# Moving the memory side of two cross-attentions into the block before them, its second layer's share into the recurrence's chunk loop

## The chip, the cores and the metric

The kernel runs on one core of a Trainium2 chip. The metric is the device time of one execution in microseconds (us); lower is better. Engines are named as in the profile: PE (TensorE), PEld (its weight loads), DVE (VectorE), ACT (ScalarE), POOL (GpSimd, which issues most of the small DMAs here) and SP (SyncE, which issues the stream of weights).

## The reference, cut to what matters

Two networks run one after the other on 256 tokens of width 2048. The second has two layers; each has a mixer, a cross-attention to a fixed memory of 256 rows, and a feed-forward part.

```
for layer in range(2):
    xn = rms_norm_2(x, norm_mix[layer])
    mix = even block (sparse attention + rwkv7) @ even_w_out   if layer == 0
          s5 block @ odd_w_out                                 if layer == 1
    x = x + mix
    x = x + memory_cross_attention(rms_norm_2(x, norm_xattn[layer]),
                                   rms_norm_2(mem, norm_mem[layer]), wq, wkv, wo)
    x = x + squared_relu_mlp(rms_norm_2(x, norm_ffn[layer]), w_up, w_down)

def memory_cross_attention(xn, memn, wq, wkv, wo):
    q  = (xn @ wq)        # 256 x 512
    kv = (memn @ wkv)     # 256 x 1024: keys and values, 4 heads of 128 each
    ...softmax attention of q over kv...
    return o @ wo
```

`memn @ wkv` depends on the inputs alone: not on x, nor on anything computed earlier.

## The kernel before, in words

**Weights.** Each large product is a `Gemm`: chunks of 512 output columns (`c`), two tiles of 128 tokens (`t`), and slots (`s`) of 256 rows of weights. SP streams the slots of all Gemms in the order of the list `gemms` (`ORDER`) into a ring of 8 (`ring`, 512 KB each, L524), eight ahead of their use. A slot has two halves: SP writes the raw weights into half 1. For a Gemm with `split=True`, ACT (`round_hi`, L1409) writes a rounded copy into half 0 and DVE (`take_lo`, L2017) the rest into half 1, and PE makes three products of each block: high by high, high by low and low by high (L841). With `split=False` PE makes one float32 product from the raw half, and half 0 of the slot isn't used.

**Streams.** ACT and DVE walk through a Gemm with `stream`: at each slot `s` of chunk `c` they round or split the slot that lies 8 ahead; at the last slot, `s == g.slots - 1`, they first call a hook that empties the accumulation banks of chunk `c` (`empty` on ACT, `hook` on DVE, as in `residual`, L2150).

**The even block.** After its input product come three small float32 Gemms (`uq`, `qidx`, `uv`), the sparse attention (`dsa_units`; the index scores are at L1112, and DVE then picks the top 64 by eight rounds of MAX8), and the recurrence `rwkv`. DVE first mixes each token with the one before (`w_sh`, shifted copies that POOL loads by DMA, L2742 to L2748), then come two passes over 128 tokens (low-rank products L1135, running sums L1140, exponentials, transposes L896), the gate (L1158, L1159), and the 32x32 matrices of all 8 chunks of 32 tokens, which DVE inverts (the solve, L2836 to L2844). Last is the loop over the 8 chunks (`heads`, L1171): PE and DVE hand each other z, u and the state, and PE's products all have 32 or 64 rows and columns. Then comes `even_out`, a split Gemm.

**The cross-attention `xat(l)`.** PE runs `xq` (one chunk, 8 slots, split); POOL has loaded the memory (`memb`), ACT sums its squares, DVE scales a diagonal by the inverse root (`norm_diag`), and PE turns the memory with it (`turn_normed`, L898, 64 products of 128x128), DVE and ACT splitting the result into `feat`. Then PE runs `xkv` (two chunks, 16 slots, split: 192 products of 128x512), turns q and k (L896), and attends. `xo` brings the result back to x. The attention waits for the semaphore `xqk_ready`, which ACT raises behind its whole stream (L1834).

Of the kernel before, what the change touches and what calls it, by code (L numbers as in the profile page):

```python
# [30 lines left out]
ACT = mybir.ActivationFunctionType  # L31
# [5 lines left out]
P = 128  # L37
# [6 lines left out]
KS = 2  # L44
# [132 lines left out]
def two_blocks(nc, I, out):  # L177
    ctx = ExitStack()
    with ctx:
# [74 lines left out]
        q_d = dram("q_d", (2 * SEQ, B1_HALF))  # L254
        s_bd = dram("s_bd", (4, P, 2048))
# [43 lines left out]
        memb = view(20480, TT, D)  # L299
        diag = view(30464, TT, P)  # L300
# [54 lines left out]
        g.append(Gemm("uv", flat(W("dsa_w_uv_2", 0)), 256, chunks(0, 1024), 2, "act_free", split=False))  # L355
        g.append(Gemm("even_out", W("even_w_out_2", 0), D, chunks(0, D), 2, "dve_free", unroll=True))
# [61 lines left out]
        d_ckt = view(29984, 2, SEQ)  # L418
        d_kid = view(0, TT, P)
# [156 lines left out]
        def _(pool):  # L576
# [51 lines left out]
            for l in range(2):  # L628
# [24 lines left out]
                dma(gates[l][0:8, 0], g_d[l].rearrange("j c d -> (j c) d"), "g8_in")  # L653
# [6 lines left out]
            pool.wait_ge(sem("x_norm_even"), L.due("x_norm_even"))  # L660
# [8 lines left out]
            pool.wait_ge(sem("even_h"), L.due("even_h"))  # L669
            pool.wait_ge(sem("dsa_part"), L.due("dsa_part", 5))  # L670
# [20 lines left out]
            dma(w_g2a[:, 0], I["rwkv_g2_2"][0, 0:P], "g2_in")  # L691
            dma(w_g2a[0:32, 1], I["rwkv_g2_2"][0, P:160], "g2_in")
# [22 lines left out]
            for o in range(2):  # L715
                dma(w_tt[64 * o:64 * o + RC], by_unit[o], "t_in")
# [16 lines left out]
            for l in range(2):  # L733
                if l == 1:
# [4 lines left out]
                    pool.wait_ge(sem("x_norm_odd"), L.due("x_norm_odd"))  # L739
# [15 lines left out]
                pool.wait_ge(sem("mem_free"), L.due("mem_free"))  # L755
                dma(memb, I["mem_2"][0].rearrange("(t p) d -> p t d", p=P), "mem_in")
# [5 lines left out]
        def _(pe):  # L762
# [161 lines left out]
            def turn_normed(src, tiles=TT, on=diag):  # L924
# [111 lines left out]

            def block1(l):
# [6 lines left out]
                pe.wait_ge(sem("sgu_in"), 16 * (l + 1))  # L1044
# [20 lines left out]
                pe.wait_ge(sem("g8_in"), 16 * (l + 1))  # L1065
# [15 lines left out]
            def even():  # L1081
                g_in, g_uq, g_qi, g_uv, g_out = gemms["even"]
# [19 lines left out]
                for t in range(TT):  # L1102
# [3 lines left out]
                    for h in (0, 4):  # L1106
                        turn([d_qi[:, t, (h + j) * P:(h + j + 1) * P] for j in range(4)])
                pe.wait_ge(sem("dsa_part"), E.due("dsa_part"))
                for t in range(TT):
                    for hp in range(8):  # L1110
                        bank = begin("act_free")
                        pe.matmul(bank[:, :], d_qit[:, hp, t * P:(t + 1) * P], d_kit, start=True, stop=True) \  # L1112
                            .then_inc(sem("unit_full"), E.up("unit_full"))
                pe.wait_ge(sem("bias_ready"), E.due("bias_ready"))
# [11 lines left out]
            def rwkv():  # L1126
                pe.wait_ge(sem("rwkv_in"), 16 * 7)
                for t in range(TT):
# [17 lines left out]
                    mm.then_inc(sem("unit_full"), E.up("unit_full"))  # L1146
                    pe.wait_ge(sem("arbk_ready"), E.due("arbk_ready"))
# [3 lines left out]
                pe.wait_ge(sem("g2_in"), 32)  # L1151
# [35 lines left out]
                within(0)  # L1187
                for c in range(NRC):
# [11 lines left out]
                    if c == 0:  # L1200
                        pe.wait_ge(sem("t_in"), 32)
# [5 lines left out]
                    heads("act_free", lambda hp, o: state(hp, o, 1) + [(w_G[c % 2][two[o], hp, 1, :], kbv[two[o], 1, hp, :])])  # L1207

            def xat(l):
                g_q, g_kv, g_o = gemms[f"xat{l}"]  # L1210
                g_prev = gemms["odd" if l else "even"][-1]
                gemm(g_q, feat_lhs(feat), parts=True, between=(3, lambda: turn_x(g_prev, x4, 3)))
                turn_normed(memb)
                gemm(g_kv, feat_lhs(feat), parts=True)
                pe.wait_ge(sem("xqk_ready"), E.due("xqk_ready"))
                for t in range(TT):
                    turn([xa_q[:, t, j * P:(j + 1) * P] for j in range(4)])
                    turn([xa_kv[:, t, j * P:(j + 1) * P] for j in range(4)])
# [45 lines left out]
            def odd():  # L1264
# [3 lines left out]
                def turn_end():  # L1268
                    turn_x(g_prev, x4, 3)
                    E.seen["rstd_ready"] = 3  # L1270
# [112 lines left out]
        def _(act):  # L1383
# [28 lines left out]
            def stream(g, empty=None, counts=(), unroll=False, each=None):  # L1412
# [4 lines left out]
                def chunk(c, i):  # L1417
                    for s in range(g.slots):
                        if s == g.slots - 1 and empty:
                            empty(c, i)  # L1420
# [211 lines left out]

            def s5_natural():
# [101 lines left out]
            def even():  # L1735
                g_in, g_uq, g_qi, g_uv, g_out = gemms["even"]

                def to_hb(c, cs, t, bank):
# [12 lines left out]
                    .then_inc(sem("act_free"), E.up("act_free")))  # L1751
                evac(g_qi, lambda c, cs, t, bank: f(d_qi[:, t, c * CH:(c + 1) * CH], bank, ACT.Copy) \
# [11 lines left out]
                act.nop().then_inc(sem("kt_ready"), E.count("kt_ready"))  # L1764
                slots = [stage[:, 0], stage[:, 1], prob[:, 0], prob[:, 1]]
# [7 lines left out]
                act.wait_ge(sem("rl_used"), E.due("rl_used", 4))  # L1773
                attend(dsa_units())

                for t in range(TT):
                    if t == 0:
# [5 lines left out]
                        .then_inc(sem("lora_ready"), E.up("lora_ready"))  # L1783
                    skip("unit_full", 4)
# [15 lines left out]
                    f(w_t[:, 0], w_t[:, 0], ACT.Exp, scale=-DECAY).then_inc(sem("eexc_ready"), E.up("eexc_ready"))  # L1800
                act.wait_ge(sem("kbv_out"), E.due("kbv_out", 16 * 6 * TT))
# [8 lines left out]
                for c in range(NRC):  # L1810
# [1333 lines left out]
```

## Time and profile before

| | |
|---|---|
| median of 3 runs | 4608.1 us (4605.08 to 4614.41) |
| the profiled execution's own time | 4608.53 us, span 4606.7 us, 1.8 us around it |
| PE busy | 4047.0 us, 88% of the span |
| DVE / ACT / POOL busy | 2283.0 / 1666.4 / 134.4 us |
| mean granted TensorE clock | 0.922 |
| DMA | 717.12 MB, mean 156 GB/s |

The page gives busy time by engine and, in 40 slices of 115 us, shares and the granted clock. A timeline gives instructions in order; its bracket is the idle time of that engine ahead of them and what ended it. One float32 product of 512 columns shows as two records. Times inside the span count from its start.

### The profile page before, as it was taken

Reading aid. Unit: us, or ns where it says so; the run is one execution under the profiler, and the core shown is the slowest. Engines: PE = TensorE matmul, PEld = TensorE weight load, DVE = VectorE, ACT = ScalarE, POOL = GpSimd, SP = SyncE. Lnnn points to the kernel's source line nnn. Section 1 sums busy time; section 2 is a strip of 40 time slices with the busy share of each in tenths; the row PEclk is TensorE's granted clock in tenths of the full one; section 3 lists DMA queues with packets and bytes.
Section 4 is the critical chain, followed back from the end, with each engine's and each line's share of the span. In section 5 each row is a group of like instructions: output and inputs, shape, how many; then the busy total and the mean of one; then the engine's idle time right before and its main releaser. Section 6 shows DMA issues by size and latency. Waiting matters only on the chain. (4 is left out here: it accounts for less than half of the span.)

```text
span 4606.7 us, 52925 instructions
## 1 busy us (share of the span) xinstructions
PE 4047.0 (88%) x21471; PEld 3175.4 (69%) x21471; DVE 2283.0 (50%) x3339; ACT 1666.4 (36%) x2235; POOL 134.4 (3%) x241
## 2 busy tenths in 40 slices
PE   6699999699798999633878999999986898999999
PEld 3466657568687787322657788788875777887887
DVE  6611223553555654665365555455546455554554
ACT  4121212331343443310024454354442454543543
POOL 1000000000000000012100000000000000000000
PEclk8899999899999999855689999999988999999999
DMA  9465554213364375221145466665651554666665
GB/s 355 182 209 196 201 179 136 69 69 95 101 202 126 102 215 176 72 72 40 30 129 169 132 185 190 183 186 188 225 175 52 174 178 129 186 188 183 187 197 163
DMA packets 350199, 717.12 MB, mean 156 GB/s; under 512 B 24270, under 2 KB 26666, under 8 KB 344602
## 3 DMA queue, kind: packets, MB, share of 16 engines
q1 hardware_dynamic: 331872, 637.74, 44.9%
q0 software_dynamic: 17600, 76.35, 5.0%
q8 instruction: 145, 2.38, 0.2%
q14 instruction: 62, 0.51, 0.0%
q10 hardware_dynamic: 520, 0.14, 0.0%
HBM read 686.33 MB, written 24.38 MB: 154 GB/s over the span
## 5 line engine op out<-in xcount | busy, mean ns | idle before, releaser
L2017 DVE TENSOR_TENSOR ring_r<-ring,ring_r 128x1024 fp32r<-128x1024 f32 (+1 forms) x1016 | 1231.7, 1219 | 1835.7 <-ACT ring_r L1409 1816.4
L1409 ACT ACTIVATE ring_r<-ring 128x1024 fp32r<-128x1024 f32 (+1 forms) x1016 | 1065.8, 1054 | 1987.8 <-DMA ring<-in_w_in 656.0
L841 PE MATMUL acc<-ring_r,feat_hi 128*128 128x512 f32 x5376 | 1689.6, 396 | 53.4 <-DVE big L2150 17.0
L841 PEld LDWEIGHTS acc<-ring_r,feat_hi 128*128 128x128 f32 x5376 | 1011.4, 190 | 318.6 <-DVE ring_r L2017 42.0
L841 PE MATMUL acc<-ring_r,feat_lo 128*128 128x512 f32 x2688 | 1055.6, 393 | 0.0
L841 PE MATMUL acc<-ring_r,hid_t_hi 128*128 128x512 f32 x2048 | 631.5, 389 | 0.0
L841 PEld LDWEIGHTS acc<-ring_r,feat_lo 128*128 128x128 f32 x2688 | 510.0, 190 | 109.1
L841 PEld LDWEIGHTS acc<-ring_r,hid_t_hi 128*128 128x128 f32 x2048 | 383.7, 188 | 79.3
L841 PE MATMUL acc<-ring_r,hid_t_lo 128*128 128x512 f32 x1024 | 398.5, 389 | 0.0
L841 PE MATMUL acc<-ring_r,feat_e_hi 128*128 128x512 f32 (+1 forms) x1088 | 329.5, 386 | 13.6 <-DVE feat_e_lo L3074 8.0
L896 PE MATMUL tp<-ident,big 128*128 128x128 f32 (+1 forms) x591 | 99.5, 329 | 161.6 <-DVEq L2806 33.5
L841 PEld LDWEIGHTS acc<-ring_r,feat_e_hi 128*128 128x128 f32 x1088 | 203.3, 190 | 54.1 <-issue 8.2
L841 PEld LDWEIGHTS acc<-ring_r,hid_t_lo 128*128 128x128 f32 x1024 | 192.2, 188 | 39.8
L1171 PE MATMUL acc<-big 64*32 64x64 f32 (+3 forms) x2208 | 144.7, 280 | 85.1 <-DVEq L2865 51.8
L841 PE MATMUL acc<-ring_r,feat_e_lo 128*128 128x512 f32 (+1 forms) x544 | 209.5, 385 | 0.0
L896 PEld LDWEIGHTS tp<-ident,big 128*128 128x128 f32 (+1 forms) x591 | 85.8, 171 | 178.0 <-issue 37.2
L1171 PEld LDWEIGHTS acc<-big 64*32 64x32 f32 (+2 forms) x2208 | 110.4, 155 | 120.7 <-issue 87.0
L781 PE MATMUL tp<-ring,silu_c 128*32 128x512 f32 x512 | 122.6, 600 | 0.0
L841 PEld LDWEIGHTS acc<-ring_r,feat_e_lo 128*128 128x128 f32 x544 | 103.1, 190 | 20.4
L898 PE MATMUL tp<-big 128*128 128x128 f32 x384 | 58.5, 315 | 54.9 <-DVEq L2055 29.9
L898 PEld LDWEIGHTS tp<-big 128*128 128x128 f32 x384 | 53.9, 225 | 60.1 <-DVEq L2055 31.2
L939 PE MATMUL acc<-big 128*128 128x256 f32 (+1 forms) x160 | 66.5, 507 | 26.2 <-DVEq L2721 22.0
(436 smaller groups left out, 3198.3 us busy)
## 6 DMA issues: line engine op xcount, KB each, us to landing
ring<-in_ffn_up SPq DMA_DIRECT2D x256, 512.0 KB, 3.7
ring<-in_ffn_down SPq DMA_DIRECT2D x256, 512.0 KB, 3.7
ring<-in_w_mod SPq DMA_DIRECT2D x192, 512.0 KB, 5.6
ring<-in_w_in SPq DMA_DIRECT2D x176, 512.0 KB, 3.8
ring<-in_w_out SPq DMA_DIRECT2D x64, 512.0 KB, 3.6
ring<-in_even_w_in SPq DMA_DIRECT2D x64, 512.0 KB, 3.6
ring<-in_even_w_out SPq DMA_DIRECT2D x32, 512.0 KB, 3.6
ring<-in_xattn_wkv SPq DMA_DIRECT2D x32, 512.0 KB, 3.6
```

Source lines behind the costliest of these rows:

```text
L781: return pe.matmul(bank[at:at + 32, :], silu_c[:, kk, :], ring[:, slot, 1, k, :], start=(kk < 4), stop=(kk >= g.kt - 4))
L841: mm = pe.matmul(bank[0:l.shape[-1], 0:width], l, r, start=(kk == 0 and j == 0), stop=(kk == g.kt - 1 and j == len(terms) - 1))
L896: mm = pe.transpose(bank[0:b.shape[-1], j * P:j * P + b.shape[0]], b, ident[0:b.shape[0], 0:b.shape[0]])
L898: mm = pe.matmul(bank[:, j * P:(j + 1) * P], b, scale, start=True, stop=True)
L939: pe.matmul(bank[:, 0:u["k"].shape[-1]], u["q"], u["k"], start=True, stop=True) \
L1171: mm = pe.matmul(banks[o][64 * o + at:64 * o + at + rows_out, hp * n:(hp + 1) * n], lt, rhs, start=(j == 0), stop=(j == len(terms) - 1))
L1409: f(ring_r[:, slot, 0, 0:kt, 0:width], ring[:, slot, 1, 0:kt, 0:width], ACT.Copy) \
L2017: tt(lo, raw, hi, ALU.subtract).then_inc(sem("w_lo"), E.up("w_lo"))
```

## The change

- `xkv0` and `xkv1` move from `xat0` and `xat1` into `gemms["even"]`, behind `uv` and ahead of `even_out`, and are no longer split. They are done in eight units (`mem_kv(l, c, t)`: layer, 512 columns, 128 rows of memory) of 16 float32 products each. A unit takes eight slots of the ring; the unit with `t == 1` frees them.
- The memory is loaded once, when the even block's input product is done, into the unused half 0 of ring slots 4 to 7 (`mem_raw`). PE turns it twice (`turn_mem`: 32 transposes), and ACT scales it by `norm_mem{l}` into half 0 of slots 0 to 3 (`mem_turned`). The scale by the inverse root (`mem_rstd`) is applied when ACT empties a unit. The result goes to DRAM (`kv_d`) by a DMA on ACT's queue.
- Layer 0's units stand: behind the index scores (0,0,0); between the sparse attention and the recurrence (0,0,1) and (0,1,0); in the recurrence's first pass behind its running sums (0,1,1). The second `turn_mem` stands behind the second pass. Layer 1's four units stand in the chunk loop, one at the end of each of chunks 0 to 3.
- Because half 0 of the ring is taken, ACT and DVE round and split the first eight slots of `even_out` in chunks 4 to 7 of the loop, two in each.
- DVE makes `within(0)` ahead of the solve and not behind it.
- In `xat(l)` only `xq` and `xo` are left. `xa_kv` is loaded from `kv_d`; k is turned at slot 5 of `xq` and copied by ACT at slot 6.
- In every Gemm the hook of `stream`, on ACT and DVE, comes at slot `slots - 2`, one slot earlier.
- Some semaphores are merged (`sgu_in`, `rwkv_in`, `x_normed`).

```diff
+        g += [Gemm(f"xkv{l}", W("xattn_wkv_2", l), D, chunks(0, 1024), 2, "act_free", split=False) for l in range(2)]
         g.append(Gemm("even_out", W("even_w_out_2", 0), D, chunks(0, D), 2, "dve_free", unroll=True))
...
-            g.append(Gemm(f"xkv{l}", W("xattn_wkv_2", l), D, chunks(0, 1024), 2, "act_free"))
...
+        mem_raw = lambda t, h: ring[:, 4 + 2 * t + h, 0].rearrange("p q n -> p (q n)")
...
POOL
             pool.wait_ge(sem("even_h"), L.due("even_h"))
+            for t in range(TT):
+                for h in range(2):
+                    dma(mem_raw(t, h), I["mem_2"][0, t * P:(t + 1) * P, h * 1024:(h + 1) * 1024], "mem_in")
...
-                pool.wait_ge(sem("mem_free"), L.due("mem_free"))
-                dma(memb, I["mem_2"][0].rearrange("(t p) d -> p t d", p=P), "mem_in")
+                dma(xa_kv, kv_d[l].rearrange("(t p) d -> p t d", p=P), "mem_in")
...
PE
+            def mem_kv(l, c, t):
+                g = gemms["even"][4 + l]
+                bank = begin("act_free")
+                for s in range(g.slots):
+                    slot = (g.q0 + c * g.slots + s) % RING
+                    pe.wait_ge(sem(f"ring_full{slot}"), ...)
+                    for k in range(KS):
+                        kk = KS * s + k
+                        mm = pe.matmul(bank[:, :], mem_feat(kk)[:, t * P:(t + 1) * P], ring[:, slot, 1, k, :],
+                                       start=(kk == 0), stop=(kk == g.kt - 1))
+                    if t == TT - 1 and s < g.slots - 1:
+                        mm.then_inc(sem("ring_free"), E.up("ring_free"))
...
+                    if t == 0:
+                        turn_mem()
...
+                mem_kv(0, 0, 0)
                 pe.wait_ge(sem("bias_ready"), E.due("bias_ready"))
                 attend(dsa_units())
+                mem_kv(0, 0, 1)
+                mem_kv(0, 1, 0)
                 rwkv()
...
                     heads("act_free", lambda hp, o: state(hp, o, 1) + [(w_G[c % 2][two[o], hp, 1, :], kbv[two[o], 1, hp, :])])
+                    if c < 2 * TT:
+                        mem_kv(1, c // TT, c % TT)
...
-                gemm(g_q, feat_lhs(feat), parts=True, between=(3, lambda: turn_x(g_prev, x4, 3)))
-                turn_normed(memb)
-                gemm(g_kv, feat_lhs(feat), parts=True)
+                gemm(g_q, feat_lhs(feat), parts=True, between=(3, lambda: turn_x(g_prev, x4, 3)), each=turn_k)
...
ACT and DVE, in stream
-                        if s == g.slots - 1 and hook:
+                        if s == max(g.slots - 2, 0) and hook:
...
+                    for s in range(2 * (c - 2 * TT), 2 * (c - 2 * TT) + 2) if c >= 2 * TT else ():
+                        take_lo(g_out.q0 + s)
```

**PE, the end of chunk 0 and the start of chunk 1 of the recurrence's loop, before.** The rows are the products with u (64x64, the state), those of the output, and the z products of the next chunk; the loop's products all carry the line of `heads`.

```order
L1171 MATMUL acc<-big 64x64 [waits dve_free,zu_ready]
L1171 MATMUL acc<-big 64x64 x15
L1171 MATMUL acc<-big 32x64 [waits dve_free]
L1171 MATMUL acc<-big 32x64 x15
L1171 MATMUL acc<-big 32x64 [waits dve_free,st_ready,G_ready,kbv_in1]
L1171 MATMUL acc<-big 32x64 x31
```

And the same place in the change:

```order
L1218 MATMUL acc<-big 32x64 [waits dve_free]
L1218 MATMUL acc<-big 32x64 x15
L1056 MATMUL acc<-ring 128x512 [waits ring_full2,dve_free]
L1056 MATMUL acc<-ring 128x512
...
L1056 MATMUL acc<-ring 128x512 [waits ring_full1]
L1056 MATMUL acc<-ring 128x512
L1218 MATMUL acc<-big 32x64 [waits dve_free,st_ready,act_free,G_ready,kbv_in1]
L1218 MATMUL acc<-big 32x64 x31
```

Sixteen products of 128x512 stand between the output's products and the next chunk's z; the same in the three chunks that follow, and in chunks 4 to 7 nothing.

**PE, between the last product of the sparse attention and the first transposes of the recurrence, before:**

```order
L954 MATMUL acc<-big,prob_t 128x128 [waits dve_free,prob_turned]
L954 MATMUL acc<-big,prob_t 128x128
L896 MATMUL tp<-ident,big 64x128 [waits prob_turned,lora_ready,rwkv_in]
L896 MATMUL tp<-ident,big 64x128
L1135 MATMUL acc<-big 128x512 [waits dve_free,lora_t]
L1135 MATMUL acc<-big 128x512 [waits dve_free] x3
```

And in the change:

```order
L1056 MATMUL acc<-ring 128x512 [waits ring_full0]
L1056 MATMUL acc<-ring 128x512
L1056 MATMUL acc<-ring 128x512 [waits ring_full1]
L1056 MATMUL acc<-ring 128x512
L1056 MATMUL acc<-ring 128x512 [waits ring_full2,dve_free]
L1056 MATMUL acc<-ring 128x512
...
L1056 MATMUL acc<-ring 128x512 [waits ring_full1]
L1056 MATMUL acc<-ring 128x512
L904 MATMUL tp<-ident,big 64x128 [waits prob_turned,lora_ready,rwkv_in]
L904 MATMUL tp<-ident,big 64x128
```

Two units, 32 products, stand ahead of the recurrence's transposes (shown: the end of the first, the start and the end of the second); the second waits for the same slots anew, which SP can only refill as the first one frees them.

## Rows read from the trace of the kernel before

**Rows 1.** The page: busy time of TensorE and ScalarE, and the ring's DMA queue.
```profile
PE 4047.0 (88%) x21471; PEld 3175.4 (69%) x21471; DVE 2283.0 (50%) x3339; ACT 1666.4 (36%) x2235; POOL 134.4 (3%) x241
...
q1 hardware_dynamic: 331872, 637.74, 44.9%
```

**Rows 2.** Groups of PE between 2464.5 and 2525.5 us: busy, mean, idle before.
```profile
L841 PE MATMUL acc<-ring_r,feat_hi 128*128 128x512 f32 x128 | 39.5, 390 | 0.0
L841 PE MATMUL acc<-ring_r,feat_lo 128*128 128x512 f32 x65 | 25.3, 389 | 0.0
L898 PE MATMUL tp<-big 128*128 128x128 f32 x64 | 9.7, 324 | 7.6 <-DVE big L2072 6.1 <-DVEq L2055 1.4
```

**Rows 3.** Timeline of PE in the first cross-attention: start, us, what, [idle before].
```profile
2452.62 1.03 PE L896 MATMUL tp<-ident,big 128*128 128x128 f32 x8
...
2465.98 3.84 PE L898 MATMUL tp<-big 128*128 128x128 f32 x32 [1.43 <-DVEq L2055]
...
2530.19 3.67 PE L896 MATMUL tp<-ident,big 128*128 128x128 f32 x16 [4.78 <-ACTq L1834]
2534.70 2.07 PE L939 MATMUL acc<-big 128*128 128x256 f32 x4 [0.84 <-DVEq L2948]
```

**Rows 4.** Timeline of PE in the second cross-attention.
```profile
3758.99 3.84 PE L898 MATMUL tp<-big 128*128 128x128 f32 x32 [0.69 <-DVEq L2055]
...
3823.46 3.68 PE L896 MATMUL tp<-ident,big 128*128 128x128 f32 x16 [4.75 <-ACTq L1834]
```

**Rows 5.** Timeline of PE where the feed-forward's first and second halves begin.
```profile
2584.22 1.22 PE L841 MATMUL acc<-ring_r,feat_hi 128*128 128x512 f32 x2 [3.87 <-DVE big L2150]
...
2948.09 1.22 PE L841 MATMUL acc<-ring_r,feat_hi 128*128 128x512 f32 x2 [4.75 <-DVE big L2150]
```

**Rows 6.** Timeline of PE: float32 products of 512 columns (two records each).
```profile
1887.30 14.00 PE L1112 MATMUL acc<-big 128*128 128x512 f32 x32 [0.84 <-DVEq L2686]
...
1992.70 3.42 PE L1140 MATMUL acc<-big,tri 128*128 128x512 f32 x4 [2.88 <-ACT big L1787]
...
2066.28 2.07 PE L1158 MATMUL acc<-big 128*128 128x512 f32 x2 [0.63 <-DVEq L2819]
```

**Rows 7.** Stretches: PE, PEld, DVE, ACT, POOL busy, PEclk, DMA share, GB/s.
```profile
1904.00:1922.00 18.00, 0.00 (x0) 0.00 (x0) 16.70 (x47) 2.39 (x4) 0.00 (x0) 0.50 0.00 0
1954.00:1981.00 27.00, 0.00 (x0) 0.00 (x0) 25.40 (x14) 0.74 (x3) 4.74 (x9) 0.51 0.71 180
...
2014.00:2018.00 4.00, 3.32 (x16) 3.32 (x17) 2.41 (x4) 0.00 (x0) 2.60 (x3) 0.50 0.28 61
...
2020.00:2022.00 2.00, 0.95 (x9) 0.68 (x7) 2.00 (x4) 0.00 (x0) 0.77 (x1) 1.00 0.98 281
...
2103.00:2149.00 46.00, 0.00 (x0) 0.00 (x0) 38.90 (x64) 0.00 (x0) 6.47 (x13) 0.50 0.10 29
```

**Rows 8.** Timeline of PE in the recurrence's two passes.
```profile
1982.64 7.19 PE L1135 MATMUL acc<-big 64*128 64x512 f32 x8 [0.63 <-DVEq L2761]
...
2014.68 6.27 PE L896 MATMUL tp<-ident,big 128*128 128x128 f32 x34 [16.88 <-DVEq L2806]
2022.22 3.70 PE L1135 MATMUL acc<-big 64*128 64x512 f32 x8 [1.27 <-DVEq L2761]
```

**Rows 9.** DMA between 1950 and 1985 us: queue share, then issues with time to landing.
```profile
q0 software_dynamic: 1056, 4.87, 54.7%
...
big<-big POOLq DMA_DIRECT2D x1, 1666.9 KB, 10.3
...
big<-in_rwkv_a POOLq DMA_DIRECT2D x1, 256.0 KB, 18.8
```

**Rows 10.** Timeline of DVE: the first instruction that reads the second shifted copy.
```profile
1965.49 2.28 DVE L2742 TENSOR_TENSOR big<-big 128x2048 f32<-128x2048 f32 x1
```

**Rows 11.** Timeline of PE: two of the chunk loop's runs without a gap.
```profile
2187.62 16.94 PE L1171 MATMUL acc<-big 64*64 64x64 f32 x224 [1.53 <-DVEq L2879]
...
2230.79 14.73 PE L1171 MATMUL acc<-big 64*64 64x64 f32 x224 [1.53 <-DVEq L2879]
```

More of the change, by code:

```diff
@@ L733, in _ @@
             for l in range(2):
-                if l == 1:
+                if l == 0:
+                    pool.wait_ge(sem("mem_free"), L.due("mem_free"))
+                    for j in range(2):
+                        pool.wait_ge(sem(f"kv_out{j}"), 16 * 4)
+                else:
                     pool.wait_ge(sem("s5_free"), L.due("s5_free"))
@@ L1035, in _, with turn_mem @@
                     piece()
+            def mem_kv(l, c, t):
+                nonlocal q
+                g = gemms["even"][4 + l]
+                bank = begin("act_free")
+                for s in range(g.slots):
+                    use = g.q0 + c * g.slots + s
+                    slot = use % RING
+                    pe.wait_ge(sem(f"ring_full{slot}"), 16 * (use // RING + 1))
+                    for k in range(KS):
[4 more added lines that the diff above has]
+                        mm.then_inc(sem("ring_free"), E.up("ring_free"))
+                mm.then_inc(sem("gemm_full"), E.up("gemm_full"))
+                if t == TT - 1:
+                    q += g.slots
+            def turn_mem():
+                pe.wait_ge(sem("mem_in"), 16 * 4)
+                for k in range(0, KT, 2):
+                    n, bank = tp_bank("act_tp")
+                    for j in range(2):
+                        for t in range(TT):
+                            at, cols = (2 * j + t) * P, (k + j) % 8 * P
+                            mm = pe.transpose(bank[:, at:at + P], mem_raw(t, (k + j) // 8)[:, cols:cols + P], ident[:, :])
+                    to_act(n, mm)
             def block1(l):
@@ L1081, in even @@
             def even():
[L1082 removed]
+                g_in, g_uq, g_qi, g_uv, g_kv0, g_kv1, g_out = gemms["even"]
                 g_prev = gemms["b1_1"][-1]
@@ L1418, in chunk @@
                     for s in range(g.slots):
-                        if s == g.slots - 1 and empty:
+                        if s == max(g.slots - 2, 0) and empty:
                             empty(c, i)
@@ L1630, in project, with mem_sums, mem_turned, mem_kv @@
                     evac(n, keep_zb)
+            def mem_sums():
+                act.wait_ge(sem("mem_in"), 16 * 4)
+                for t in range(TT):
+                    junk, src = (ring[:, at:at + 2, 0].rearrange("p s q n -> p s (q n)") for at in (2 * t, 4 + 2 * t))
+                    f(junk, src, ACT.Square, accum_out=stat[:, 76 + t:77 + t]).then_inc(sem("act_step"), E.up())
+                act.wait_ge(E.last_sem(), E.last_count())
+                f(stat2[:, 76:78], stat[:, 76:78], ACT.Sqrt, bias=eps[:, 1:2], scale=1.0 / D).then_inc(sem("sd_ready"), E.up("sd_ready"))
+            def mem_turned(l):
+                for k in range(0, KT, 2):
+                    bank = take_turn()
+                    for j in range(2):
+                        name = "act_tp" if j else "act_step"
+                        f(mem_feat(k + j), bank[:, j * SEQ:(j + 1) * SEQ], ACT.Copy, scale=col(f"norm_mem{l}")[:, k + j:k + j + 1]) \
+                            .then_inc(sem(name), E.up(name))
+                act.wait_ge(sem("act_step"), E.cnt["act_step"])
+                act.wait_ge(E.last_sem(), E.last_count())
+                act.nop().then_inc(sem("mem_feat"), E.count("mem_feat"))
+            def mem_kv(l, c, t):
+                n = (l * 2 + c) * TT + t
+                dst = hb[:, n % 2, 0:CH]
+                if n >= 2:
+                    act.wait_ge(sem(f"kv_out{n % 2}"), 16 * (n // 2))
+                f(dst, take("gemm_full"), ACT.Copy, scale=mem_rstd[:, t:t + 1]).then_inc(sem("act_free"), E.up("act_free"))
+                act.wait_ge(E.last_sem(), E.last_count())
+                act_dma(kv_d[l, t * P:(t + 1) * P, c * CH:(c + 1) * CH], dst, f"kv_out{n % 2}")
             def s5_natural():
```

148 lines of the change are left out of this document (93 added, 55 removed).

## The prediction

> **What bounds the kernel now.** I read the page first: PE is busy 88% of the span, DVE 50%, ACT 36% [rows 1]. Most of the time is PE multiplying streamed weights, so a product taken off PE's line there is worth its full duration. The second view is PE's timeline with its groups, at the two cross-attentions. The reader is to see that between the end of `xq` and the wait for `xqk_ready` PE has hardly a gap: 192 products (128 rows with `feat_hi`, 65 with `feat_lo`, one of them from outside) take 39.5 + 25.3 us, the turning 9.7, and only 7.6 us are idle [rows 2]. So the memory side lies wholly on the path. The third view is the stretches of the even block: there DVE works while PE stands still at a granted clock of 0.50, or 1.2 GHz [rows 7]. The last is the chunk loop, where PE runs 224 small products without a gap [rows 11]; PE and the hand-overs bound it, and a unit put in there is paid for. The question is what comes off at full clock and what goes on at which clock.
>
> The sum is made against the profiled execution's own 4608.5 us; the median of the runs shown is 4608.1, so no correction is needed.
>
> **1. The memory side leaves the cross-attention: −121.3.** In layer 0 the stretch runs from 2465.98 − 1.43 to 2530.19 − 4.78, 60.9 us [rows 3]; in layer 1 from 3758.99 − 0.69 to 3823.46 − 4.75, 60.4 us [rows 4]. The 4.8 us wait for `xqk_ready` stays: ACT raises it behind its last slots in either kernel.
>
> **2. Turning q and k: −1.3.** Now only q's 8 transposes follow, half of the 16 in 3.67 us, and two of the four copies after them go: −1.7 per layer. k's transposes move into `xq`, where 8 cost 1.03 [rows 3]: +1.03. Twice −0.65 is −1.3. Loading `xa_kv` is hidden by `xq`; if that cover fails, some 10 us per layer, the landing time of POOL's copy in [rows 9].
>
> **3. The hook one slot earlier: −10.** At the start of the feed-forward's first half PE waits 3.87 us for DVE's addition, at the second 4.75 [rows 5]. The addition now comes ahead of the last slot's split. I take 2.4 to 2.7 of each such wait, four in all. Bounds: 5 (half of that) and 16 (all but a microsecond of each). Elsewhere the order of two short steps changes; from −3 to +3, taken as 0.
>
> **4. Unit (0,0,0) behind the index scores: 0.** Sixteen products of this shape took 14.00 us at full clock, 0.875 each [rows 6]. Between 1904 and 1922 PE does nothing while DVE picks the top 64 [rows 7]; a start at half clock makes it 16. If that cover were gone: +16. Two turnings of the memory (32 transposes took 3.84 [rows 3]) stand in waits too; 0 to +6 each, taken as 0, since ACT loses more work than it gains there.
>
> **5. The pair (0,0,1), (0,1,0): +7.** It needs 2 × 14.0 = 28 us; PE is idle from 1954 to 1981 [rows 7], 27 us: +1. But the second unit waits for slots that are refilled only as the first frees them: 8 × 512 KB = 4.19 MB. By the ring's row, 637.74 MB take 44.9% of 4606.7 us [rows 1], or 3.24 us per MB, so 13.6 us of all 16 DMA engines. In these same 35 us the shifted copies and `in_rwkv_a` already use 54.7% [rows 9], 19.1 us. Together 32.7 against 27: +5.7. What is late then is DVE's mix: the copy lands 10.3 us after issue, and DVE reads it at 1965.49 [rows 10], so there is no slack; the low-rank transposes wait for it. Bounds: 0 (the transfers fit in between) and +14 (the refill is all added). I take +7, as both use the whole set of engines at the same time.
>
> If each queue had engines of its own, this term would be +1 and the sum 6 lower. The Trainium skill, "DMA: Bandwidth & Descriptors", section "Issuing engines are not separate DMA queues", says that DMAs from any engine end on the same 16 and interleave, which speaks against this place for the pair; the trace so far shows only the share of 0.71 without the ring.
>
> **6. The first pass at full clock: −4.** L1135 takes 7.19 us in the first pass and 3.70 in the second [rows 8]; the first now comes behind 28 us of dense products, so −3.5, and −0.5 for the transposes around it. Bounds 0 and −6. Unit (0,1,1) takes 14 to 16 us, where PE waits 16.88 us for DVE [rows 8]: 0; its refill is 13.6 us more of DMA, with nothing large beside it.
>
> **7. The gate's products: −2.** A product of L1158 took 2.07 us at half clock [rows 6]; some of the sixteen now follow the second turning of the memory. Bounds 0 and −6.
>
> **8. Four units in the loop: +55.6.** The unit stands on PE behind the output's products and ahead of the next chunk's z; ahead of these there is no gap [rows 11], DVE is waiting for them, so the unit delays the whole chain. Its price hangs on the clock. At full clock 14.0 us. At half, L1140's two products took 3.42, 1.71 each [rows 6]. When PE began with transposes at 2014.68 [rows 8], the clock was 0.50 up to 2018 and 1.00 from 2020 [rows 7]: it rose after some 4.2 us. In 4.2 us 2.46 products are done, the other 13.54 take 11.85: 16.1 us. Against that, the products behind a unit run at full clock for a while: the loop's runs of 224 took 16.94 or 14.73 us [rows 11], by how much of each was at full clock, so −2.2. Per chunk 13.9, four times 55.6. Bounds: 44 (the unit starts warm and 3 us are given back) and 64.4 (16.1, nothing given back).
>
> The solve would have room, 46 us without PE [rows 7], but no unit stands there. `within(0)` ahead of it costs nothing: DVE and the way of T through DRAM decide there. Rounding the first slots of `even_out` in chunks 4 to 7 is hidden, since ACT and DVE wait for PE in the loop.
>
> **Sum:** −121.3 − 1.3 − 10 + 0 + 7 − 4 − 2 + 55.6 = −76. **Forecast: 4532 us**, its own range 4500 to 4560.
>
> **Rivals.**
> - **B, the clock is carried through.** For it: the loop's runs get faster by themselves at times [rows 11], and a unit adds dense work. Then a unit costs 14.0 and gives back twice 2.2: 4 × 9.6 = 38, or **4514**. Against it: every chunk has hand-overs during which PE waits (1.53 us before each run). Chance 0.12.
> - **A, the clock doesn't rise in the units.** They stand as bursts between small dependent products. Each costs 16 × 1.71 = 27.4, the loop 109.6, 54 more: **4586**. Against it: dense transposes raised the clock within 4.2 us [rows 7, 8]. Chance 0.08.
> - **C, slower than before: the float32 product of a streamed block costs what L1158's does, 2.07 us**, wherever PE comes out of small products, as it does there for 17 us on end [rows 6]. A unit is then 33.1 us. The loop is +132.4, 77 more than above; (0,0,0) no longer fits 18 us, +17; the pair is 66 against 27, +32; (0,1,1) is over by 16. Together −76 + 142 = +66: **4674**. It decides from a product of about 1.5 us on: 128 products stand behind 76 us of gain, 0.6 each above 0.9. Against it: the 14.00 us of L1112. Chance 0.03.
> - **D, the change doesn't do what it says for the cross-attention**: `xa_kv`, issued behind POOL's other loads, lands late, 10 us in each layer: **4552**. Chance 0.02.
>
> Rival A has a rule on its side: the Trainium skill, "TensorE: Matmul & The Clock Gate", section "HAM oscillation — how this bites in real kernels", tells of matmuls in bursts parted by waits, which fall back to the slow clock before every burst and so do much of their work cold. The trace agrees as far as the half clock at 2014 goes. By it one unit per chunk pays the slow start four times, where four in a row would pay once; by the 16.1 and 14.0 above that is 6 us of my sum, and 54 if no burst ever gets warm.
>
> **How the numbers follow.** The forecast has 0.75. Its range, widened to take in B and the near part of A, is 4500 to 4568; outside lie most of A, C, and tails of the rest, 2 in 10 at most. A measurement of this kernel can tell 0.2%, 9 us, from no change. Faster by more: forecast, B, A and D, 0.96. Within 9 us: 0.01, only a mixture of A and a bad pair. Slower: C, 0.03.
>
> **What would show it.** In the changed profile: no L898 in the cross-attentions, and `xo` some 15 us behind `xq` rather than 75; PE's waits at the feed-forward's starts 1 to 2 us; chunks 0 to 3 of the loop longer than 4 to 7 by 14 us, with a unit's 32 records over 15 to 17 us and the clock going from 0.50 to 1.00 inside it; DVE's mix stretched between 1954 and 1990, with the DMA share near 1. I am wrong in term 8 if a unit takes 14 or 27; in term 5 if the recurrence's first transposes come as early as before or more than 14 us later; in term 1 if a wait for `xa_kv` stands ahead of k's transposes.

## The result and the profile after

The changed kernel takes **4500.2 us** (median of 4 runs, 4497.6 to 4503.0) against 4607.5 us for the one before (4605.1 to 4614.4): a ratio of 0.9765, 95% interval 0.9748 to 0.9782. It is faster by 107 us, where 76 were forecast; the forecast of 4532 us is 32 us too high, and the lower end of the range, 4500, is about where the measurement lies. The profiled execution took 4502.98 us, its span 4501.2.

The page's rows that answer to [rows 1]:

```profile
PE 4046.3 (90%) x21279; PEld 3129.9 (70%) x21279; DVE 2219.7 (49%) x3266; ACT 1639.7 (36%) x2218; POOL 136.8 (3%) x245
...
q1 hardware_dynamic: 331872, 637.74, 45.6%
```

PE is busy as long as before, 4046.3 us against 4047.0, so by the page the 105 us are idle time. (Inside the busy sum the units added, the products gone and the products that no longer run at half clock cancel; the mean granted clock rose from 0.922 to 0.932.) To see where they went, I compare the starts of the same steps in the two timelines of PE:

| step | before | after | gained so far | by this stretch |
|---|---|---|---|---|
| float32 products of the even block (uq) | 1833.15 | 1816.01 | 17.1 | 17.1 |
| index scores | 1887.30 | 1868.17 | 19.1 | 2.0 |
| sparse attention | 1923.31 | 1905.08 | 18.2 | −0.9 |
| recurrence's first transposes | 1981.40 | 1973.16 | 8.2 | −10.0 |
| its first small products | 2083.62 | 2072.78 | 10.8 | 2.6 |
| end of chunk 0's hand-over | 2165.07 | 2154.78 | 10.3 | −0.5 |
| even_out | 2349.91 | 2392.09 | −42.2 | −52.5 |
| xo, layer 0 | 2553.95 | 2534.20 | 19.7 | 61.9 |
| first feed-forward, first half | 2584.22 | 2561.68 | 22.5 | 2.8 |
| the same, second half | 2948.09 | 2920.09 | 28.0 | 5.5 |
| s5 block's glu product | 3535.53 | 3496.25 | 39.3 | 11.3 |
| xo, layer 1 | 3847.23 | 3748.30 | 98.9 | 59.6 |
| second feed-forward, first half | 3875.84 | 3774.15 | 101.7 | 2.8 |
| the same, second half | 4238.59 | 4132.88 | 105.7 | 4.0 |

The chunk loop, PE's timeline in the changed kernel (start, us, what, [idle before]); it answers to [rows 11]:

```profile
2154.78 3.82 PE L1218 MATMUL acc<-big 64*64 64x64 f32 x64 [1.52 <-DVEq L2997]
2158.53 14.69 PE L1056 MATMUL acc<-ring 128*128 128x512 f32 x32
2173.15 11.37 PE L1218 MATMUL acc<-big 64*32 64x64 f32 x128
...
2189.23 5.30 PE L1218 MATMUL acc<-big 64*64 64x64 f32 x96 [1.52 <-DVEq L2997]
2194.45 14.00 PE L1056 MATMUL acc<-ring 128*128 128x512 f32 x32
2208.39 11.96 PE L1218 MATMUL acc<-big 64*32 64x64 f32 x128
...
2229.47 14.00 PE L1056 MATMUL acc<-ring 128*128 128x512 f32 x32
...
2263.35 14.00 PE L1056 MATMUL acc<-ring 128*128 128x512 f32 x32
```

The units run at full clock or nearly: three take 14.00 us, the first 14.69. Straight ahead of each, without a gap, stand 3.8 to 5.3 us of small products. The granted clock was 0.50 when these began, and 1.00 when the second, third and fourth unit began; ahead of the first unit it was still 0.50, and it rose within that unit.

The pair behind the attention, in the same view:

```profile
1933.32 13.90 PE L1056 MATMUL acc<-ring 128*128 128x512 f32 x32
1950.13 1.95 PE L1056 MATMUL acc<-ring 128*128 128x512 f32 x4 [2.92 <-DMA ring<-in_xattn_wkv]
1954.33 3.01 PE L1056 MATMUL acc<-ring 128*128 128x512 f32 x4 [2.25 <-DMA ring<-in_xattn_wkv]
1960.19 13.14 PE L1056 MATMUL acc<-ring 128*128 128x512 f32 x24 [2.85 <-DMA ring<-in_xattn_wkv]
1973.16 0.38 PE L904 MATMUL tp<-ident,big 128*64 128x128 f32 x2
```

PE waits three times for the ring, 8.0 us in all, and goes on with the transposes without a gap. These waits cost clock too. The stretches of the pair and of the loop's first two units (PE, PEld, DVE, ACT, POOL busy, PEclk, DMA share, GB/s):

```profile
1933.50:1973.00 39.50, 31.49 (x64) 12.70 (x64) 25.66 (x14) 2.68 (x5) 4.76 (x9) 0.87 0.79 236
2158.50:2173.20 14.70, 14.70 (x35) 6.40 (x34) 0.42 (x1) 1.18 (x2) 4.14 (x8) 0.95 0.16 36
2194.40:2208.40 14.00, 14.00 (x38) 6.01 (x33) 0.00 (x0) 1.18 (x2) 4.11 (x8) 1.00 0.79 235
```

The clock was 1.00 up to the end of the second wait and 0.50 from 1957.3 to 1964.2, so the sixteen products of the second unit took 18.1 us (1.95, 3.01 and 13.14) and not 14.0. The recurrence's transposes come 39.7 us after the attention's end, 12.1 later than in the kernel before: 8.0 of waits and 4.1 of slower products. And PE comes last here; DVE isn't late. Its mix, to which [rows 10] belongs, and ACT behind it, in the same stretch:

```profile
1946.66 2.29 DVE L2857 TENSOR_TENSOR big<-big 128x2048 f32<-128x2048 f32 x1 [1.40 <-DMA big<-big]
...
1954.31 7.37 DVE L2863 TENSOR_TENSOR big<-big 128x2048 f32<-128x2048 f32 x4
1973.65 0.42 DVE L2873 COPY big<-tp 64x256 f32<-64x256 f32 x1 [11.97 <-PE tp L904]
```
```profile
1961.77 0.56 ACT L1874 ACTIVATE big<-big 128x160 f32<-128x160 f32 x2 [12.13 <-DVEq L2866]
1962.24 0.24 ACT L1876 ACTIVATE big<-big 128x64 f32<-128x64 f32 x1
```

DVE waited 1.4 us for its shifted copy; everything that the transposes read was there at 1962.5, 29 us after the attention, and PE came 10.7 us later.

Last, the first network, where nothing of the memory was moved. This group of PE's products with its idle time, from 445 us up to the first scaled transposes of its second block, before and after (columns: busy, mean ns, idle before and what ended it):

```profile
L841 PE MATMUL acc<-ring_r,feat_hi 128*128 128x512 f32 x1400 | 444.0, 399 | 27.5 <-DVE modc L2399 13.2 <-ACT prob L1704 7.5 <-DVE stage L2576 4.0
```
```profile
L849 PE MATMUL acc<-ring_r,feat_hi 128*128 128x512 f32 x1400 | 440.2, 396 | 15.0 <-DVE modc L2505 14.0 <-ACT big L1681 1.0
```

12.5 us of waits are gone, and 3.8 of busy time. L1704 and L2576 are lines that hooks call, where a Gemm's banks are emptied (L1681 too, in the changed kernel). Behind such a wait PE's products ran at half clock first, as here before the change: pairs of records of 1.05 us and single ones of 0.63, then 0.62 and 0.39.

```profile
649.31 1.19 PE L841 MATMUL acc<-ring_r,feat_hi 128*128 128x512 f32 x2 [3.73 <-ACT prob L1704]
650.30 0.63 PE L841 MATMUL acc<-ring_r,feat_lo 128*128 128x512 f32 x1
650.73 1.05 PE L841 MATMUL acc<-ring_r,feat_hi 128*128 128x512 f32 x2
...
654.41 0.62 PE L841 MATMUL acc<-ring_r,feat_hi 128*128 128x512 f32 x2
654.87 0.39 PE L841 MATMUL acc<-ring_r,feat_lo 128*128 128x512 f32 x1
```

ACT's timeline at this wait, before:

```profile
641.08 1.06 ACT L1409 ACTIVATE ring_r<-ring 128x1024 fp32r<-128x1024 f32 x1 [6.68 <-DMA ring<-in_w_in]
642.05 1.29 ACT L1704 ACTIVATE prob<-acc 128x512 f32<-128x512 f32 x2
648.57 0.60 ACT L1704 ACTIVATE prob<-acc 128x512 f32<-128x512 f32 x1 [5.23 <-DMA q_d<-prob]
650.29 0.60 ACT L1704 ACTIVATE prob<-acc 128x512 f32<-128x512 f32 x1 [1.12 <-DMA q_d<-prob]
```

And after:

```profile
633.12 0.60 ACT L1793 ACTIVATE prob<-acc 128x512 f32<-128x512 f32 x1 [4.03 <-PE acc L849]
634.51 0.60 ACT L1793 ACTIVATE prob<-acc 128x512 f32<-128x512 f32 x1 [0.79 <-PE acc L849]
637.65 0.60 ACT L1793 ACTIVATE prob<-acc 128x512 f32<-128x512 f32 x1 [2.54 <-DMA q_d<-prob]
638.44 0.60 ACT L1793 ACTIVATE prob<-acc 128x512 f32<-128x512 f32 x1 [0.19 <-ACT prob L1793]
```

Before, full banks stood behind a rounding that waited 6.68 us for its load; a load is only asked for when PE leaves a slot, near the end of the same chunk. After, ACT waits for PE's product itself and empties the banks one by one, their DMA leaves earlier, and ACT has the fourth free at 639.0 instead of 650.9. Some 3.3 us of these 11.9 the changed kernel was ahead already at the chunk's start; over the chunk it gained 5.2 (60.8 us against 66.1 between the starts of its products and of the next chunk's).

### The profile page after: what moved, and what is told of

It reads as the page before. It is cut to its first block and busy times, and to the rows that moved or that the text cites. A ratio compares the mean times of both kernels' runs of the same rounds, so it can differ in the third digit from the quotient of the medians.

```text
span 4501.2 us, 52469 instructions
## 1 busy us (share of the span) xinstructions
PE 4046.3 (90%) x21279; PEld 3129.9 (70%) x21279; DVE 2219.7 (49%) x3266; ACT 1639.7 (36%) x2218; POOL 136.8 (3%) x245
## 5 line engine op out<-in xcount | busy, mean ns | idle before, releaser
L2123 DVE TENSOR_TENSOR ring_r<-ring,ring_r 128x1024 fp32r<-128x1024 f32 (+1 forms) x984 | 1190.2, 1219 | 1694.7 <-ACT ring_r L1467 1675.1
L1467 ACT ACTIVATE ring_r<-ring 128x1024 fp32r<-128x1024 f32 (+1 forms) x984 | 1030.8, 1055 | 1811.9 <-DMA ring<-in_w_in 589.4
L849 PE MATMUL acc<-ring_r,feat_hi 128*128 128x512 f32 x5120 | 1601.4, 394 | 31.6 <-DVE modc L2505 14.0
L849 PEld LDWEIGHTS acc<-ring_r,feat_hi 128*128 128x128 f32 x5120 | 958.0, 189 | 282.5 <-DVE ring_r L2123 35.2
L849 PE MATMUL acc<-ring_r,feat_lo 128*128 128x512 f32 x2560 | 1001.2, 391 | 0.0
L849 PEld LDWEIGHTS acc<-ring_r,feat_lo 128*128 128x128 f32 x2560 | 483.6, 189 | 102.9
L1218 PEld LDWEIGHTS acc<-big 64*32 64x32 f32 (+2 forms) x2208 | 108.9, 154 | 121.3 <-issue 46.4
L1056 PE MATMUL acc<-ring 128*128 128x512 f32 x256 | 121.6, 635 | 14.7 <-DMA ring<-in_xattn_wkv 8.0
L1056 PEld LDWEIGHTS acc<-ring 128*128 128x128 f32 x256 | 51.1, 204 | 80.8 <-issue 72.2
L849 PE MATMUL acc<-ring_r,s_zhi 128*128 128x512 f32 x256 | 80.8, 397 | 7.9 <-DVE big L3169 7.9
```

Of the source, the lines that this page charges most:

```text
L849: mm = pe.matmul(bank[0:l.shape[-1], 0:width], l, r, start=(kk == 0 and j == 0), stop=(kk == g.kt - 1 and j == len(terms) - 1))
L1056: mm = pe.matmul(bank[:, :], mem_feat(kk)[:, t * P:(t + 1) * P], ring[:, slot, 1, k, :], start=(kk == 0), stop=(kk == g.kt - 1))
L1218: mm = pe.matmul(banks[o][64 * o + at:64 * o + at + rows_out, hp * n:(hp + 1) * n], lt, rhs, start=(j == 0), stop=(j == len(terms) - 1))
L1467: f(ring_r[:, slot, 0, 0:kt, 0:width], ring[:, slot, 1, 0:kt, 0:width], ACT.Copy) \
L2123: tt(lo, raw, hi, ALU.subtract).then_inc(sem("w_lo"), E.up("w_lo"))
```

## The experiments

Eleven runs. Medians are in us; the kernel before ran beside each group (medians 4610.8, 4609.0 and 4607.8 for the three groups). Each kernel starts from the changed one unless it says otherwise.

**Does the hook carry the missing gain?** The hook back at its old slot in the changed kernel, on both engines:

```diff
-                        if s == max(g.slots - 2, 0) and empty:
+                        if s == g.slots - 1 and empty:
...
-                        if s == max(g.slots - 2, 0) and hook:
+                        if s == g.slots - 1 and hook:
```

> The changed kernel (4500.2 us), only with the hook of stream back at slot slots - 1 on ACT and DVE. Theory 1, the earlier hook made the part of the gain that the prediction lacked: it gave 15.1 us at the four starts of the feed-forward's halves, 19.1 ahead of the index scores (2.0 of them between the small Gemms) and about 10 in the second layer's s5 block, so this kernel takes 4500 + 44 = 4544 us. Theory 2, the gain outside the feed-forward comes from the merged semaphores or the freed buffers: only the 15 come back, 4515 us. In the trace theory 1 wants the waits of 1.2 to 3.8 us for ACT and DVE inside the first network's products back.

Measured 4543.8 (4541.9 to 4545.6), ratio to before 0.9852, 0.9836 to 0.9867. The same two lines the other way round in the kernel before, and nothing else of the change:

> The kernel before (4607.5 us), only with the hook one slot earlier on ACT and DVE, nothing moved. Theory 1: 4607.5 - 44 = 4563 us. Theory 2: 4607.5 - 15 = 4592 us. If the hook helps only beside the moved products, 4600 or more.

Measured 4558.3 (4557.9 to 4564.3), ratio 0.9884, 0.9869 to 0.9900. Theory 1 holds from both sides. The hook is worth 44 us by the first (4543.8 against 4500.2) and 52 by the second (4558.3 against the 4610.8 beside it), 4 to 5 tenths of the whole gain, and the rest of the change 64 to 67; the median of the kernel before itself differs by 3 us between the groups. The traces of the kernel before and of `hook_only` say where: 16.3 us up to `uq`, 16.4 at the four starts of the feed-forward, 12.8 between the first feed-forward's second half and the s5 block's glu product, of 44.2 in all. The 2.0 us between `uq` and the index scores are not the hook's, although the expectation counted them so: this stretch is 54.15 us long before, 52.16 in the changed kernel and 52.14 in `hook_back`. The waits inside the first network came back in `hook_back` as they had been, and are gone in `hook_only` (second row):

```profile
L849 PE MATMUL acc<-ring_r,feat_hi 128*128 128x512 f32 x1402 | 444.1, 398 | 28.3 <-DVE modc L2505 13.1 <-ACT prob L1793 8.6 <-DVE stage L2682 3.8
```
```profile
L841 PE MATMUL acc<-ring_r,feat_hi 128*128 128x512 f32 x1400 | 439.3, 395 | 16.0 <-DVE modc L2399 15.1 <-ACT big L1623 1.0
```

**Where does it act, and on which engine?** Late only for Gemms ahead of `uq`, early behind:

```diff
-                        if s == max(g.slots - 2, 0) and empty:
+                        if s == (max(g.slots - 2, 0) if g.q0 >= gemms["even"][1].q0 else g.slots - 1) and empty:
```

(and the same for DVE's hook).

> The changed kernel with the hook back at the last slot in the Gemms of the first network and the even block's input product, early from uq on. The trace of the changed kernel stood 17.1 us ahead of the one before at the end of the even block's input product; if the earlier hook made all of that, this kernel takes 4500.2 + 17.1 = 4517 us. Rival: these 17 us are a matter of the startup and of the waits for the inputs, and the hook gave its 44 us behind: 4500 to 4504.

Measured 4509.1 (4506.2 to 4517.2), ratio 0.9780, 0.9762 to 0.9798. The profiled execution is the slowest of the four, 4517.2; in its timeline `uq` starts at 1830.65, 14.6 us later than in the changed kernel's. So the first network's part is there, and the rival is out, but its size is 9 by the medians and 15 by these two traces. All traces together narrow it: in the eight with the hook one slot earlier in this network `uq` starts between 1810.2 and 1820.5, in the three with both engines' hooks at the old slot (before, `hook_back` and this one) between 1830.7 and 1835.0. The means are 18 us apart, and the same code alone spreads over 10.

> The changed kernel with ACT's hook back at the last slot and DVE's left early. Theory 1 (each engine empties its own banks late, so the gain divides by whose bank PE waits for): the feed-forward's 15 us, which are DVE's additions, stay; the waits for ACT in the first network (10.3 us in the rows of before, some of them with a restart at half clock) and those of the s5 block (about 10 us) come back: 4500 + 20 = 4520 us, from 4514 to 4526. Theory 2 (DVE's take_lo waits for ACT's rounding anyway, so the one is worth nothing without the other): all 44 come back, 4544.

Measured 4523.2 (4519.4 to 4536.0), ratio 0.9810, 0.9792 to 0.9828: 23 us of the 44 come back with ACT's hook alone. PE's waits at the feed-forward's starts stay short (1.36 to 1.99 us), since DVE's hook makes that addition. In the trace, whose execution was the slowest of the four at 4536.0, `uq` starts 20.8 us later than in the changed kernel and the stretch to the s5 block's glu product is 14.5 us longer. So the gain divides by whose bank PE waits for. DVE's hook alone at the old slot wasn't run.

**Is still earlier better?** The hook at `slots - 3` on both engines:

> The changed kernel with the hook at slot slots - 3. Theory 1 (the late hook stood behind a rounding that waits for a load of 3.7 us, which is freed one slot of 2.7 or 5.4 us before the chunk's end; at slots - 2 the rounding ahead of the hook is through before the end): nothing is left to gain, 4498 to 4503 us, and the waits ahead of the feed-forward stay at 1.1 to 2.2 us. Theory 2 (the earlier the better, DVE has a standing backlog): another 5 to 10 us go, 4490 to 4495. Theory 3 (three slots' roundings pushed behind the hook come late for PE): slower than 4505.

Measured 4503.7 (4498.1 to 4507.2), ratio 0.9779, 0.9764 to 0.9794. No gain shows, although two of the four waits ahead of the feed-forward fell to 0.78 us in its trace. At that slot the kernel's output is not the reference's, and where it goes wrong wasn't traced: its time is a hint that nothing is left to gain, not more.

**What does a unit cost where PE isn't on the path?** Layer 1's four units out of the loop, behind `within(0)`:

```diff
                 within(0)
                 pe.wait_ge(sem("mem_feat"), E.due("mem_feat"))
+                for n in range(2 * TT):
+                    mem_kv(1, n // TT, n % TT)
                 for c in range(NRC):
...
-                    if c < 2 * TT:
-                        mem_kv(1, c // TT, c % TT)
```

(ACT's calls and DVE's skips follow.)

> The changed kernel with layer 1's four units on PE right behind within(0), ahead of the loop, and none in the loop. In the changed kernel's trace the loop's units cost 52.2 us, and PE is idle or waiting from 2091.5 to 2151.3 but for 4.8 us of small products. Theory 1 (a unit costs the loop its whole time because PE is on the path there, and nothing where DVE solves): four units of 14.0 us and about 3 us for the refill of the slots end some 4 us late: 4500 - 52 + 4 = 4452 us, from 4448 to 4458. Theory 2 (the refill of eight slots between the second and third unit costs 8 us or more, as in the pair): 4460 us. Theory 3 (the loop's clock was kept up by the units and drops back): the loop gives 6 us less, 4458 us or more, to be seen in runs of 224 products at 16.9 us instead of 14.7.

Measured 4450.3 (4441.3 to 4451.3), ratio 0.9645, 0.9627 to 0.9662: 50 us faster than with the units in the loop. PE's timeline there:

```profile
2088.20 56.46 PE L1056 MATMUL acc<-ring 128*128 128x512 f32 x128 [0.40 <-issue]
2144.59 2.10 PE L1218 MATMUL acc<-big 32*32 32x64 f32 x64
2147.25 0.70 PE L1218 MATMUL acc<-big 64*32 64x32 f32 x32 [0.56 <-DVE big L2989]
2154.60 1.92 PE L1218 MATMUL acc<-big 32*32 32x64 f32 x32 [6.65 <-DMA big<-t_d]
```

Four units in 56.46 us, without a wait for the ring between the second and the third, which rules out theory 2. Theory 3 isn't seen either: the loop is 52.7 us shorter, and its runs of 224 small products take 14.7 to 16.9 us, as in the kernel before. Still, the stretch ahead of the loop is 6.9 us longer: PE waits 6.65 us for T. Its way through DRAM is longer, as the DMA issues show (KB each, us to landing), in the changed kernel and in this one:

```profile
t_d<-big POOLq DMA_DIRECT2D x1, 512.0 KB, 2.9
big<-t_d POOLq DMA_DIRECT2D x2, 256.0 KB, 5.8
```
```profile
ring<-in_even_w_out SPq DMA_DIRECT2D x8, 512.0 KB, 6.7
...
t_d<-big POOLq DMA_DIRECT2D x1, 512.0 KB, 6.7
big<-t_d POOLq DMA_DIRECT2D x2, 256.0 KB, 9.6
```

**Was it PE or the mix that came late behind the pair?** Only (0,0,1) stays behind the attention; (0,1,0) goes to the first pass, (0,1,1) to the second:

```diff
                 mem_kv(0, 0, 1)
-                mem_kv(0, 1, 0)
                 rwkv()
...
-                    if t == 0:
-                        mem_kv(0, 1, 1)
+                    mem_kv(0, 1, t)
```

> The changed kernel with unit (0,1,0) moved from the pair to the first pass of the recurrence and (0,1,1) from the first pass to the second. In the changed kernel the recurrence's first transposes come 39.7 us after the attention's end, with 8.0 us of waits for the ring inside the second unit, while DVE and ACT have their input ready after 29. Theory 1 (PE itself, with its wait for the ring's refill, is what was late): the transposes come 29 us after the attention, 10.7 earlier: 4500.2 - 10.7 = 4489.5 us, less if a unit overruns the 16.2 us idle time of the second pass (up to 2 us). Theory 2 (the forecast's: DVE's mix is late because its shifted copy shares the DMA engines): the mix still waits, and only a few us go, 4496 to 4500 us.

Measured 4485.0 (4484.0 to 4493.1), ratio 0.9731, 0.9717 to 0.9746: 15 us faster. The transposes wait for their input again and start 29 us after the attention's end (1927.52):

```profile
1927.52 13.47 PE L1056 MATMUL acc<-ring 128*128 128x512 f32 x31
1956.55 0.60 PE L904 MATMUL tp<-ident,big 128*64 128x128 f32 x2 [15.57 <-issue]
```

Of these 15 us, the even block from the index scores to even_out shows 8.2 in the two traces (10.8 at the transposes, and 2.6 lost again behind them); the rest lies within what stretches with the same code differ by.

**Both together, and the last 7 us.** `hold_even_out` adds one wait on SP:

```diff
                             for h in [g] + g.riders:
+                                if g.name == "even_out" and (c, s) == (0, 0):
+                                    sp.wait_ge(sem("rwkv_in"), 16 * 11)
                                 if q >= RING:
```

> Both moves in one kernel: the pair split over the two passes and layer 1's four units behind within(0). Each alone gave 4485.0 and 4450.3 against 4500.2. If they add up, 4450.3 - 15.2 = 4435 us (by the traces 10.7 to 15). If the slots that (0,1,1) frees in the second pass come too late for the first unit of layer 1, or the loads of the gate's weights are delayed, 4440 to 4445.

> split_and_solve, and SP waits with the first load of even_out until T has come back from DRAM. With the units behind the solve, T's way from the solve's end to PE took 18.8 us instead of 12.0 in the changed kernel: its write 6.7 us instead of 2.9 and its read 9.6 instead of 5.8, while 4.19 MB of even_out were being loaded. If the shared DMA engines cause that, the way is 12 us again and the kernel 5 to 7 us faster than split_and_solve, 4429 us. If the way is long for another reason (DVE's z copy stands behind the units), the time stays. The weights themselves are first needed in chunk 4, 80 us later, so the hold costs nothing.

Measured 4441.7 (4437.5 to 4443.5), ratio 0.9634, 0.9619 to 0.9650, and 4440.4 (4439.8 to 4442.6), ratio 0.9634, 0.9619 to 0.9649. The moves add up to 58 of the 65 us (53 by the second running below). The hold did what it was meant to do in the DMA issues, T's write taking 2.9 us and its read 6.1 again, but not in the median. So both ran once more:

> The same kernel as split_and_solve, run again beside hold_even_out on one chip, since the two medians (4441.7 and 4440.4) lay closer than either kernel's own spread of 3 to 6 us: 4437 to 4444 us.

> The same kernel as hold_even_out. Its trace showed the even block, from the index scores to the first product of even_out, 6.5 us shorter than in split_and_solve (461.2 against 467.7 us). If that is what the hold is worth, the median is 6 us below split_and_solve_again. If the even_out weights that come later cost it elsewhere, the two stay within 2 us of each other, as in the first runs.

Measured 4446.9 (4439.6 to 4448.9), ratio 0.9653, 0.9640 to 0.9667, and 4436.8 (4435.5 to 4439.2), ratio 0.9630, 0.9617 to 0.9643. In these runs the hold is 10 us ahead, in the first 1 us. The mechanism showed in every trace: PE's wait at this place was 6.54 and 6.22 us without the hold, both ended by T, and 1.55 and 0.98 with it, the last ended by DVE. From the index scores to even_out the traces give the hold 6.5 us in the first pair and 6.6 in the second (467.7 to 461.2, 468.5 to 461.8); by the medians its worth for the whole kernel stays open between 1 and 10 us. The fastest kernel of the study is this last one, at 4437 to 4440 us, 60 to 63 us under the changed kernel.

## Why the prediction was wrong, point by point

- **Terms 1 and 2, the cross-attentions: right.** −121.3 and −1.3 were forecast; up to `xo` the two layers gave 61.9 and 59.6, 121.5 in all, and the transposes wait 4.83 and 4.80 us for `xqk_ready`, as was said. Only the sign "`xo` some 15 us behind `xq` rather than 75" was misread: the traces have 27 and 89 in layer 0.
- **Term 3, the hook: this is the step that failed**, at its sentence "Elsewhere the order of two short steps changes; from −3 to +3, taken as 0". The four starts of the feed-forward gave 15.1 us (forecast 10, with 16 as the bound). Elsewhere it gave 28.4 in the table: 17.1 in the first network and the even block's input product, 11.3 in the s5 block and ahead of it. The experiments put 44 to 52 us on the hook, where 10 were forecast. The two steps that change places are not short ones: one of them waits for a load. I looked for the effect only at the four waits that stood in the rows at the edges of stages, and not at the sum of the smaller waits that end with a line of a hook. The row of L841 above had much of it: 11.5 us that end with L1704 and L2576, and products at half clock behind such waits.
- **Term 4, unit (0,0,0): right**, 0.9 us instead of 0; the unit took 16.4 us, with a start at half clock, as was said.
- **Term 5, the pair: right in sign, wrong in mechanism.** +7 was forecast; +10.0 came from attention to transposes, and it would have been 12.1 if the attention ahead, which now begins at full clock, hadn't become 2.1 shorter. The DMAs that ran beside each other were behind it, but the late one was PE, waiting for the ring (8.0 us) and then at half clock (4.1), and not DVE's mix, which was late by 1.4. `pair_split` decides this. The clock behind the waits was in no term. I had added the transfers' lengths and given the delay to the consumer with no slack; the ring's loads were issued one by one as PE freed the slots and landed 21.4 us after issue, beside the large ones of POOL.
- **Terms 6 and 7: too favourable.** −6 was forecast, −2.6 came. The first pass's L1179 did run at full clock (3.70 against 7.19 us), but the gate's products still took 2.07 us each: the wait for `in_rwkv_g`'s load, 3.7 us, came between them and the turning.
- **Term 8, the loop: right in its sum, wrong in both its parts.** +55.6 was forecast, 52.5 came. The prediction itself says that it is wrong here "if a unit takes 14", and the units took 14.0 to 14.7 and not 16.1, 7.7 us less in all: the working let each start at half clock, but the clock rose before the unit began, in the small products ahead of it, three times, and early in the unit once. Behind the units the loop gave back 4.2 us and not 8.8. That the two errors nearly cancel is luck. What the term says of the path is shown: the units delay the whole chain, and taking them out of the loop made it 52.7 us shorter.
- **The rivals.** A and C asked for units of 27 and 33 us, and there are none. D didn't occur. B was right about the units of 14 us, but its time of 4514 needed 4.4 us back from each, and about 1 came. The sum missed by 30 us: 28.4 are the hook's "elsewhere" and 2.0 the small Gemms, whose cause stays open. The rest cancels (5 more at the feed-forward and 3 more at the loop; 3 less each at the pair and at terms 6 and 7, 1 less each at the cross-attentions and at term 4). The range had no bound for a change that touches every Gemm, of which there are many more than four.

The Trainium skill, "TensorE: Matmul & The Clock Gate", section "HAM oscillation — how this bites in real kernels", tells of bursts of matmuls that waits part, and that start at the slow clock again each time. The loop agrees only in part: the granted clock was at 0.50 again in the small products ahead of every unit, but these ran into the unit without a wait, and the clock was 0.95 in the first unit's stretch and 1.00 in the second's. The pair is a plain case of it: PE waited for DMAs inside the second unit, the clock fell from 1.00 to 0.50, and 4.1 us were lost.

The Trainium skill, "DMA: Bandwidth & Descriptors", section "Issuing engines are not separate DMA queues", says that DMAs started by different engines run on the same 16 DMA engines and interleave. The traces agree twice: the ring's loads of SP took 21.4 us beside POOL's in the pair, and T's write and read took 6.7 and 9.6 us beside the loads of even_out, 2.9 and 5.8 without them.

## What to carry to other kernels

An edit in a helper that every stage calls is the first thing to price, not the last: sum the waits that end with its lines over the whole program (here that would have shown much of the gain, not all of it), and ask what the emptying of a bank stands behind on its engine; if that is a wait for a load, the emptying inherits it. Move extra products to where their engine is idle and the chain is on another: the same four units cost 52 us in the loop and 7 beside the solve. And where a transfer sits on the chain, look for the bulk loads that freed buffers release beside it, and hold them if they aren't needed soon.

## What the runs showed that I had not expected

- The clock rose while PE ran only 64x64 products: behind 4.5 to 5.3 us of them without a gap, the next 128x512 unit ran at full clock from its start three times (14.00 us, the same as L1112's in [rows 6]); behind 3.8 us, once, it took 14.69. It also fell while PE had no gap: in the small products behind the first unit it was 1.00 up to 2177 and 0.50 from there to 2183.
- 4.19 MB of loads beside it lengthened a 512 KB write from 2.9 to 6.7 us and a 256 KB read from 5.8 to 9.6 us.
- The first network, with the same code, ends at times that lie up to 10 us apart in different traces (`uq` at 1810.2 to 1820.5 in eight of them); a difference of less than that between two traces says nothing about this stretch.
